# Six key projections as block products in the gate stage, six weight lows on GpSimd, and a pause of VectorE at the first power

## The reference

```
h    = rms_norm(x, norm1)
proj = h @ w_in                 # q, k, v of 8 + 8 heads, forget gate, 2048 gate columns
o_a  = forgetting_attention(qa, ka, va, log_f)      # 8 heads, causal
o_b  = chunk_band_attention(qc, kc, vc, rel_bias)   # 8 heads, a band of keys
g    = sigmoid(gates)
x    = x + (g_a * (o_a @ w_a) + g_b * (o_b @ w_b)) @ w_out
x    = x + relu(rms_norm(x, norm2) @ w_up) ** 2 @ w_down
out  = rms_norm(x, final_norm)
```

## Time and profile before

| what | value |
|---|---|
| median of 3 runs | 1803.3 us (1803.16 to 1803.54) |
| the profiled execution | 1802.78 us, of which the span is 1801.0 us |
| TensorE (PE) busy | 1784.9 us, 99% of the span |
| VectorE (DVE) busy | 1362.0 us, 76% |
| ScalarE (ACT), GpSimd (POOL) busy | 864.2 us (48%), 480.7 us (27%) |
| mean granted TensorE clock | 0.998 of full |

### The profile page before, as it was taken

One profiled execution on the slowest core, in us unless ns is written; L12 is line 12 of the kernel. 1 busy time (PEld: TensorE's weight loads), 2 busy tenths in 40 slices (PEclk: granted clock), 3 DMA queues, 4 the chain that ended last, 5 costly groups with the idle time before them and its releaser, 6 DMA issues.

```text
span 1801.0 us, 25195 instructions
## 1 busy us (share of the span) xinstructions
PE 1784.9 (99%) x8855; PEld 1500.8 (83%) x8855; DVE 1362.0 (76%) x2573; ACT 864.2 (48%) x1676; POOL 480.7 (27%) x435
## 2 busy tenths in 40 slices
PE   9999999999999999999999999999999999999998
PEld 7888888877888888888888878888888888888887
DVE  7698574888546877778888897697667678777777
ACT  6687234545334656556656434352223234344334
POOL 1110010013320000032323153016566555324223
PEclk9999999999999999999999999999999999999999
DMA  5101412333332222123216337434445477546333
GB/s 212 47 25 36 138 45 96 138 131 117 112 107 98 65 60 69 64 67 91 70 58 211 116 105 238 152 106 140 146 155 172 158 250 291 175 155 230 104 128 130
DMA packets 82684, 225.51 MB, mean 125 GB/s; under 512 B 8768, under 2 KB 16256, under 8 KB 79488
## 3 DMA queue, kind: packets, MB, share of 16 engines
q1 hardware_dynamic: 82000, 223.48, 37.2%
q10 hardware_dynamic: 560, 0.43, 0.1%
HBM read 161.45 MB, written 52.99 MB: 119 GB/s over the span
## 4 chain that ended last, share of the span: by engine, by line
PE 88%; DVE 6%; ACT 3%; issue 2%; POOL 1%; DMA 0%; POOLq 0%; DVEq 0%; ACTq 0%
PE D L1058 55%; PE S L1058 13%; PE T L1058 6%; PE PV L1423 4%; PE T L1389 3%; PE S L1361 2%; PE S L1362 2%; PE D L1099 1%; DVE xe L2106 1%; ACT SPs L2468 1%; DVE acc L1452 1%; DVE Wl L2143 1%; ACT Wh L2736 0%; PE S L1099 0%; DVE T L2236 0%
## 5 line engine op out<-in xcount | busy, mean ns | idle before, releaser
L1058 PE MATMUL D<-Hh,Wh 128*128 128x512 f32 x1052 | 277.0, 394 | 0.7 <-DVE xe L2106 0.7
L1058 PE MATMUL D<-Hh,Wl 128*128 128x512 f32 x1052 | 275.6, 393 | 0.0
L1058 PE MATMUL D<-Hl,Wh 128*128 128x512 f32 x1052 | 273.7, 392 | 0.0
L2736 ACT CAST Wh<-Wr 128x1024 fp32r<-128x1024 f32 (+2 forms) x186 | 151.4, 814 | 247.7 <-PE D L1058 184.0
L1058 PEld LDWEIGHTS D<-Hl,Wh 128*128 128x128 f32 x1052 | 194.5, 188 | 37.8
L1058 PEld LDWEIGHTS D<-Hh,Wl 128*128 128x128 f32 x1052 | 193.6, 188 | 37.3
L1058 PEld LDWEIGHTS D<-Hh,Wh 128*128 128x128 f32 x1052 | 192.5, 188 | 37.7 <-DVE xe L2106 1.1
L2143 DVE TENSOR_TENSOR Wl<-Wr,Wh 128x1024 fp32r<-128x1024 f32 (+2 forms) x179 | 181.9, 1016 | 39.9 <-ACT Wh L2736 39.4
L2736 ACT CAST Wh<-Sx 128x512 fp32r<-128x512 f32 (+1 forms) x120 | 70.5, 592 | 146.6 <-PE D L1058 79.1
L2480 ACT ACTIVATE SP<-SP,sm 128x640 f32<-128x640 f32 (+7 forms) x128 | 94.5, 738 | 64.6 <-DVE sm L1663 64.0
L2143 DVE TENSOR_TENSOR Wl<-Sx,Wh 128x512 fp32r<-128x512 f32 (+1 forms) x120 | 107.5, 903 | 22.3 <-ACT Wh L2736 21.7
(11 more groups left out here) (393 smaller groups left out, 3705.7 us busy)
## 6 DMA issues: line engine op xcount, KB each, us to landing
Wr<-w SPq DMA_DIRECT2D x62, 512.0 KB, 3.5
f_scratch<-xe SPq DMA_DIRECT2D x28, 768.0 KB, 5.2
Wr<-wdn SPq DMA_DIRECT2D x34, 512.0 KB, 4.3
Wr<-wo SPq DMA_DIRECT2D x32, 512.0 KB, 3.5
Wr<-wup SPq DMA_DIRECT2D x27, 512.0 KB, 3.8
T<-f_scratch SPq DMA_DIRECT2D x11, 1024.0 KB, 6.9
Hl<-f_scratch SPq DMA_DIRECT2D x10, 1024.0 KB, 6.6
K<-K SPq DMA_DIRECT2D x32, 256.0 KB, 3.5
```

Source lines behind the costliest of these rows:

```text
L1058: m = e.matmul(into, (low if n == 2 else high)(k), (operand_low if n == 1 else operand_high)(k), start=begin and (n, k) == todo[0], stop=( ...
L2736: e.copy(high, src).then_inc(*raised("act_weights", x))
```

## The change

Three things.

**1.** The key projections of pairs 1 to 6 (`MOVED`) leave the dense stream of the attention. They become three more block groups behind the gates (`n_gates` is 7, `n_gate_groups` now 10). ScalarE copies where it took the tanh, the results go to six more planes of `gate_scratch`, and each comes back as one 512 KB load into the row of `Wr` that the pair's raw key weights had. `query_highs`, `key_highs` and their lows read that row (`projected_rows`) in place of a PSUM bank. The row is free again when the key lows of its second half are done.

**2.** The low parts of the q and v weights of pairs 2, 3 and 4 are made on GpSimd, in its `bias` stream behind the biases of heads 3, 5 and 7; the next head's bias waits for them.

**3.** VectorE's lows and squares of the second half of x (from the third on) and the low part of the fourth of the first weights wait for the first power on GpSimd. The transposes of the first values go behind the first product of the second half.

```diff
-    gd = nc.dram_tensor("gate_scratch", (16, 128, 1024), F32, kind="Internal").ap()
+    gd = nc.dram_tensor("gate_scratch", (22, 128, 1024), F32, kind="Internal").ap()
...
-            TOGETHER += [x + (half,) for x in FIRST_IS] + [("vt", half)]
+            TOGETHER += [x + (half,) for x in FIRST_IS]
+
+        TOGETHER.insert(5, ("vt", 0))
+        TOGETHER.append(("vt", 1))
...
+        MOVED = (('k', 1), ('k', 2), ('k', 3), ('k', 4), ('k', 5), ('k', 6))
...
+                if what in MOVED:
+                    take_raw(("moved",) + what)
+                    done += [((QKV[what[0]],) + what[1:] + (half,), "moved", half) for half in halves]
+                    continue
...
-        n_gate_groups = (16 - n_plain) // 2
+        n_gates = (16 - n_plain) // 2
+        n_gate_groups = n_gates + len(MOVED) // 2
...
+        def projected_rows(x):
+            return Wr[:, raw[moved(x)], cols(x[-1])] if moved(x) in raw else psum[bank[x]][:, :]
+
+        def projected_ready(w, x):
+            w.wait_ge(*(at("ld_w", moved(x)) if moved(x) in raw else at("dense", *x)))
...
+            elif x[0] == "moved":
+                w.wait_ge(*at("dve_evac", (QKV[x[1]], x[2], 1), 1))
...
+        PAIR_ON_POOL = {pr: [("w2", kd, pr, 0) for kd in "qv" if (kd, pr) not in MOVED] for pr in range(2, 5)}
...
-                    yield from transposes(("vt", half), vt, lambda: w.wait_ge(*at("v_copied", half)))
+                        if (half, which) == (1, (0,)):
+                            yield from transposes(("vt", 0), vt, lambda: w.wait_ge(*at("v_copied", 0)))
+                yield from transposes(("vt", 1), vt, lambda: w.wait_ge(*at("v_copied", 1)))
...
+                if gen == ("x", 1) and k > 2:
+                    w.wait_ge(*at("pool_norm", "x", 0))
...
+                    if half and k > 1:
+                        w.wait_ge(*at("pool_norm", "x", 0))
...
-                        e.tensor_tensor(K[r, h, 1, cs], psum[bank[x]][r, :], K[r, h, 0, cs].bitcast(F32),
+                        e.tensor_tensor(K[r, h, 1, cs], b[r, :], K[r, h, 0, cs].bitcast(F32),
...
-                    if x not in ON_POOL + LATE_ON_POOL:
+                    if x not in ON_POOL + LATE_ON_POOL + PAIRS_ON_POOL:
...
+                        if x == FIRST[3]:
+                            w.wait_ge(*at("pool_norm", "x", 0))
...
+                        if g < n_gates:
+                            e.activation(ost, psum[bank[x]][:, :], ACT.Tanh, scale=0.5).then_inc(*raised("act_evac", x))
+                        else:
+                            e.copy(ost, psum[bank[x]][:, :]).then_inc(*raised("act_evac", x))
...
+                    if hd > 3:
+                        w.wait_ge(*at("w_lo", PAIR_ON_POOL[hd // 2][-1]))
...
+                    if s and hd > 1:
+                        w.wait_ge(*at("pool_bias", "band", hd))
+                        for x in PAIR_ON_POOL[hd // 2 + 1]:
+                            yield from weights(x, "pool_bias")
...
+                        src = w2_src(MOVED[2 * (x[1] - n_gates) + x[2]])
+                    elif kind == "moved":
+                        n = 16 + MOVED.index(x[1:])
+                        for half in both:
+                            w.wait_ge(*at("gate_spilled", n, half))
+                        src = gd[n]
```

More of the change, by code:

```diff
@@ L601, in two_block_kernel @@
         w_next[0] = (half_next[0] + 1) // 2
-        QKV2 = project([((kd, pr), both, False) for pr in range(1, 8) for kd in "qkv"])
+        ROWS2 = project([((kd, pr), both, False) for pr in range(1, 8) for kd in "qkv"])
+        QKV2 = [item for item in ROWS2 if item[1] != "moved"]
         occupy([x for x, _, _ in QKV2], D3)
@@ L848, in gates_spilled, with moved @@
         def gates_spilled(w):
-            for i in range(14, 16):
+            for i in (0, 1):
                 for half in both:
-                    w.wait_ge(*at("gate_spilled", i, half))
+                    w.wait_ge(*at("gate_spilled", n_plain + 2 * n_gate_groups - 2 + i, half))
+        def moved(x):
+            return ("moved", {"q2": "q", "k2": "k"}.get(x[0]), x[1])
+        def projected_rows(x):
+            return Wr[:, raw[moved(x)], cols(x[-1])] if moved(x) in raw else psum[bank[x]][:, :]
+        def projected_ready(w, x):
+            w.wait_ge(*(at("ld_w", moved(x)) if moved(x) in raw else at("dense", *x)))
         def pair_over(w, pr):
@@ L963, in two_block_kernel @@
         LATE_ON_POOL = (("w2", "gate", n_plain, 0), ("w2", "gate", 0, 0))
+        PAIR_ON_POOL = {pr: [("w2", kd, pr, 0) for kd in "qv" if (kd, pr) not in MOVED] for pr in range(2, 5)}
+        PAIRS_ON_POOL = tuple(x for pr in range(2, 5) for x in PAIR_ON_POOL[pr])
         def gate_ready(w, i, half):
@@ L1757, in key_lows @@
                 def key_lows(x, K, cs):
+                    b = projected_rows(x)
                     for h in range(2):
@@ L2593, in projected @@
                     if kind == "q2":
-                        w.wait_ge(*at("dense", *x))
+                        projected_ready(w, x)
                         pair_place_free(w, "q", x[1])
@@ L2837, in norms, with weights @@
                     yield 1050
-            def lows():
[L2841 to L2844, removed]
-                    e.tensor_tensor(low, src, high.bitcast(F32), ALU.subtract).then_inc(*raised("pool_weights", x))
-                    yield pool2(n)
+            def weights(x, name="pool_weights"):
+                src, high, low, n = conversion(x)
+                w.wait_ge(*at("w_hi", x))
+                also(("w_lo", x), name, x)
+                e.tensor_tensor(low, src, high.bitcast(F32), ALU.subtract).then_inc(*raised(name, x))
+                yield pool2(n)
+            def lows():
                 for x in ON_POOL:
@@ L3001, in weights_into @@
                         src = w2_src(x[1:])
+                    elif kind == "pga" and x[1] < n_gates:
+                        src = w2[24 + n_plain + 2 * x[1] + x[2]]
                     elif kind == "pga":
-                        src = w2[24 + n_plain + 2 * x[1] + x[2]]
+                        src = w2_src(MOVED[2 * (x[1] - n_gates) + x[2]])
[4 more added lines that the diff above has]
+                        src = gd[n]
                     elif kind == "pba":
@@ L3143, in group_gates_out @@
                     n += n_plain + 2 * g
-                    w.wait_ge(*at("act_evac", ("ga", g, p)))
+                    w.wait_ge(*at("act_evac" if p == 2 or g < n_gates else "dve_evac", ("ga", g, p)))
                     also(("gate_spilled", n, half), "dma_gg%d" % p, g)
```

14 lines of the change are left out of this document (8 added, 6 removed).

## The result

The changed kernel takes 1811.6 us at the median (1811.0 to 1812.1), the kernel before 1803.2 in the same comparison: a ratio of 1.0047, 95% interval 1.0035 to 1.0059. It is slower by 8.4 us, where 1795 was forecast, and above the range's upper end of 1806. The profiled execution took 1811.77 us with a span of 1810.0.

What follows compares the result with a forecast made beforehand. TensorE, busy for 1784.9 of 1801.0 us, was taken to bound the kernel. The terms -8.2 - 3.7 + 4.0 = -7.9 us, from 1802.8 or a median 0.5 us higher, gave 1795, with a range of 1789 to 1806.

Steps and rivals of the forecast that it cites:

- TensorE's work: Gate chain and attention: three more groups add 57.1 us, 288 key matmuls go for 65.3; -8.2 us.
- What the groups bring along: New gate groups: splits, sums and the key rows' DMA round trip lie beside TensorE; no cost.
- The pause: Start: with VectorE held back GpSimd's first power ends early, the 2.13 us wait and slow clock go; -3.7 us.
- What the attention loses: Attention of the first six pairs: fewer dense matmuls leave TensorE waiting for VectorE; +4 us, bounds 1 and 16.
- The lows on GpSimd: Attention: each low holds VectorE up by 0.5 us; their wait adds nothing beyond the attention's 4 us.
- the starving rival: First three pairs' ends: GpSimd lows leave TensorE 3.0 us short, plus 1.6 for the clock, each; 1809, chance 0.11.
- normalisings far over 0.5 us: Attention: sign that the forecast is wrong, VectorE's normalisings taking this long beside GpSimd's lows.
- VectorE sets the pace: Attention: each GpSimd low holds VectorE up 2.40 us; 17 us over TensorE's 274, halfway a loss of 11; chance 0.17.
- the pause does nothing: Start: the power waits for something else or postponed work is late by as much; 1799, chance 0.10.
- the case without a loss: Attention: TensorE loses nothing there; 1791, chance 0.12.

Runs made afterwards that it cites:

- start: Changed kernel without moved keys and without lows on GpSimd, so only the pause and the later transposes of the first values: 1800.0 us, ratio 0.9984.
- rows5_nolows: Changed kernel with five score rows in place of four and the six weight lows back on VectorE: 1812.1 us, ratio 1.0053.
- rows5_swap: Changed kernel with five score rows and the q projection of pair 1 moved in place of the key of pair 6: 1798.3 us, ratio 0.9974.
- rows5: Changed kernel with five score rows in place of four: 1803.3 us, ratio 1.0000.
- k4_all: Changed kernel with only the keys of pairs 1 to 4 moved, lows on GpSimd and pause kept: 1796.25 us, ratio 0.9964.
- late4_all: Changed kernel with only the keys of pairs 3 to 6 moved: 1807.7 us, ratio 1.0022.
- keys_start: Changed kernel without its lows on GpSimd, moved keys and pause kept: 1821.0 us, ratio 1.0099.

## Why the prediction was wrong, step by step

**TensorE's work: right.** 36 matmuls fewer, and a new group takes what a group took the earlier trace rows; chain of the kernel after:

```profile
555.10 19.04 PE D L1084 x84
```

**What the groups bring along: right.** The stretch with the new groups has no gap (TensorE is busy for 116.00 us from 500.0 to 616.0), and no wait for key rows that come by DMA shows among TensorE's waits.

**The pause: right in place, 0.9 us short in the end.** The first power, GpSimd's timeline of the kernel after:

```profile
22.43 1.01 POOL L2876 TENSOR_TENSOR rs_t<-ms_t,sm 128x4 f32<-128x4 f32 x1 [20.04 <-DVE ms_t L1500]
```

1.01 us in place of 3.72, the wait of 2.13 us is gone, and from 26.0 to 31.0 the clock is 1.00 where it was 0.53. The trace of start runs 3.6 us ahead up to the end of the attention and gives 0.9 back in two waits behind it (TensorE for VectorE's `xe`, 1.5 us against 1.1, and for a weight low, 0.9 against 0.4). Hence 2.8 and not 3.7.

**What the attention loses: wrong, and this is nearly the whole error.** The step put it at 4 us, with bounds of 1 and 16, and it is 20.3. Of these 12.3 us are gaps in pairs 1 to 7 (12.8 less the 0.5 of before), up to 5.1 the slow clock and 0.9 the start's return, next above, if it is here what it was in start; some 2 us aren't told apart. Three things were wrong in it:

*The share.* It took 91.6% as the share that VectorE reaches before TensorE feels it, from the last pair of before, where the output product stood beside the attention. Over the first six pairs of the kernel after VectorE reaches 87% (246.97 of 284.70 us). They shorten by 46.3 us, where the 288 matmuls that went were 66.5: a loss of 20 us in this stretch, beyond even the 16 us that the step's own upper bound gives at 88%. The round of the score rows is part of what holds VectorE there: with a fifth row and the same work it reaches 90% in pairs 1 to 3. Its own work is another part: in rows5_nolows the six lows make these pairs 7.2 us longer.

*The stretch.* The sum was made for 549.4 to 890.0 and ended two pairs before the attention does. Projections run ahead of attention, by two pairs at most. What VectorE's pace costs in the early pairs is first covered by products brought forward, and the debt falls due in the last pairs, which the sum left out: 0.9 and 1.1 us of gaps up to 897.3, then 10.8 us. rows5_swap against rows5 and k4_all against late4_all show it: with 196 and 188 projection matmuls left for the last two pairs these hardly stall, as with the 192 of before; with 148 (rows5) and 108 (the kernel after) they do. A low mean share doesn't say that VectorE is free when it is wanted: at 80% in pair 6 TensorE still stands.

*The clock.* Its fall was priced in one rival only, at a single stand of 2 us. Here it came behind gaps of 1.23, 0.40, 0.37, 0.68 and 0.56 us, with attention between them.

**The lows on GpSimd: the price of the hold was about right, but it was not free for TensorE.** They run from 656.14, 702.30 and 744.47, two at a time. Behind the first two pairs of lows TensorE has no gap, behind the third one of 0.82 us, far from the 3.0 of the starving rival. GpSimd's and VectorE's timelines there:

```profile
744.47 4.75 POOL L2884 TENSOR_TENSOR Wl<-Wr,Wh 128x1024 fp32r<-128x1024 f32 x2
747.03 2.28 DVE L1724 TENSOR_SCALAR SP<-SP,sm 128x128 f32<-128x128 f32 x1
```

A normalising of this size takes 0.29 us elsewhere (at 956.59); this one takes 2.28 and ends 0.1 us behind GpSimd. So one of the prediction's signs of being wrong, normalisings far over 0.5 us, did come. VectorE's busy time in keys_start was

```profile
PE 1789.5 (98%) x8819; PEld 1500.6 (82%) x8819; DVE 1376.8 (76%) x2603; ACT 873.8 (48%) x1697; POOL 500.1 (27%) x447
```

and 1374.3 in the kernel after: 2.5 us less for six lows that are 7.3 us of work. Of the 4.8 us between, 3.7 are in the 128 normalisings (64.6 us in keys_start, 68.3 after), some 0.6 us a low where 0.5 was taken; when the lows move alone it is 0.9 in all. The SBUF page of the Trainium skill (SBUF — State Buffer, Who interferes with whom) has it that, where a VectorE instruction in a two-port mode or with two SBUF inputs meets a GpSimd instruction that reads SBUF, the second to issue is blocked until the first has finished. The normalising of 2.28 us, which ends with GpSimd's lows, agrees with it. What was drawn from it, that the move could make VectorE's load heavier, didn't come: its busy time fell, and the lows took 9.3 us off.

**The rivals.** The slower rival (starving lows) named the wrong cause. "VectorE sets the pace" was the nearest: it had the place and the order of size (a loss of 11 to 17), and VectorE's work does count, as 7.3 us of it are worth 9.3 us with four score rows and 8.7 with five. But its reason, a hold of the full 2.40 us by each low, was wrong (some 0.6 measured), and so was the share of 91.6% that it took over from the forecast. That the time could get longer because dense products run out in the last pairs was not among the rivals. That the pause does nothing is refuted by start; the case without a loss is nearly what k4_all shows, 2 us from it, with four keys.

**A faster version.** Four keys with five score rows and the rest of the change: 1795.4 us, 7.5 us under the kernel before. What may be moved is what the attention can spare, and from the pairs that can spare it.

## What to carry to other kernels

Work that is saved on the engine that bounds the kernel is saved only as long as the engine keeps enough to do beside its waits: count the filler up to the end of the stage, and look for the point at which the filler's own sources stop it, not only at the mean over the stage. A busy share that an engine reached in one stage is no limit for another stage with other buffers and other work beside it: the latency of one round through the buffers counts too, and one more buffer shows it. An engine that runs ahead hides a loss until its filler is used up, so compare how much filler is left at the same point of both kernels. When a move gains nothing, try half of it, from one end and from the other.

## What the hardware showed that was not expected

Falls of the granted clock came behind quite different gaps. Before, it was a single stand of 2.13 us, followed by 3.4 us at 0.53. In the kernel after, 3.2 us of gaps, the longest 1.23, spread over 902.4 to 912.8, were followed by 3.4 us at 0.50; in rows5, gaps of 0.30 and 1.53 us between 958.4 and 961.0 by 13.6 us at 0.50, with 2.2 us of gaps in it. A single gap of 1.0 us (k4_all, 728.1 to 729.2) left it at 1.00, and so did 3.7 us of gaps between 638.6 and 653.9, the longest 1.34, in rows5_swap. No rule comes out of these rows. And what a GpSimd low costs VectorE depends on what stands beside it: alone, six of them took 7.3 us off VectorE's busy time, with the keys moved 2.5, and one normalising was held for 2 us.
